# A tile's normed rows in two PSUM banks, the second tile's values in the gate buffer, and thirteen resident weight chunks

## The reference

```python
h = rmsnorm(x, g_mix)
p, q, k, v, gl = split(h @ w_in)              # 512 + 3*512 + 2*1024 columns
branch_a = pool_mixer(p, w_pool, pool_scale)  # trailing means over 2/4/8/16 tokens, per-group map
branch_b = moba_attention(q, k, v) @ w_attn_up  # 8 heads of 64, causal, ALiBi
gates = sigmoid(gl)
x = x + (gates[..., :1024] * branch_a + gates[..., 1024:] * branch_b) @ w_out
xn = rmsnorm(x, g_ffn)
# PEER: per token 8 heads x 16 experts, found by two top-16 searches over 128 keys each
eid, cv = product_key_search(xn @ w_q, sub_keys)
act = gelu(einsum('thkd,td->thk', u[eid], xn))
x = x + einsum('thk,thkd->td', softmax(cv) * act, v[eid])
```

## Time and profile before

| | us |
|---|---|
| median of 3 runs | 1575.68 (1574.5 to 1578.08) |
| the profiled execution: its time | 1575.04 |
| its span, first to last instruction | 1573.3 |
| busy in the span: PE, DVE, ACT, POOL | 1284.6, 1149.6, 914.3, 662.0 |
| bytes over DMA | 643.51 MB, mean 409 GB/s |

### The profile page before, as it was taken

One profiled execution on the slowest core, in us unless ns is written; L12 is line 12 of the kernel. 1 busy time (PEld: TensorE's weight loads), 2 busy tenths in 40 slices (PEclk: granted clock), 3 DMA queues, 4 the chain that ended last, 5 costly groups with the idle time before them and its releaser, 6 DMA issues.

```text
span 1573.3 us, 18796 instructions
## 1 busy us (share of the span) xinstructions
PE 1284.6 (82%) x5582; PEld 788.0 (50%) x5582; DVE 1149.6 (73%) x2692; ACT 914.3 (58%) x3307; POOL 662.0 (42%) x516
## 2 busy tenths in 40 slices
PE   8999898886898788766688978797778888787875
PEld 8986566543554556533355546564445542222321
DVE  2159998877888869636778887976778777777545
ACT  2236566557667546434676664655676666666676
POOL 0014344455445333223554433335554445554552
PEclk9999999997999899986899989999999999999999
DMA  9979999999999999999999999999999999999997
GB/s 393 397 320 401 408 413 420 421 421 422 402 389 408 421 420 421 421 421 419 421 417 410 396 417 422 419 420 421 421 418 416 396 410 421 421 421 421 421 420 292
DMA packets 89742, 643.51 MB, mean 409 GB/s; under 512 B 9976, under 2 KB 10536, under 8 KB 11816
## 3 DMA queue, kind: packets, MB, share of 16 engines
q0 software_dynamic: 73728, 536.90, 82.8%
q1 hardware_dynamic: 15588, 105.18, 16.2%
q10 hardware_dynamic: 324, 0.23, 0.0%
HBM read 641.23 MB, written 1.05 MB: 408 GB/s over the span
## 4 chain that ended last, share of the span: by engine, by line
DMA 43%; PE 26%; DVE 18%; ACT 6%; issue 5%; POOL 2%; SPq 0%; DVEq 0%; POOLq 0%; ACTq 0%
DMA ring<-in_uv,expert 41%; PE ybank L675 13%; PE bank L476 9%; DVE ring L1181 7%; DVE xs L1194 2%; POOL ring L1316 2%; DMA wring<-in_chunks 2%; PE bank L622 1%; ACT wgt L885 1%; ACT diag L895 1%; PE bank L611 1%; ACT th L883 1%; DVE buf L974 1%; DVE picked L977 1%; DVE si L930 1%
## 5 line engine op out<-in xcount | busy, mean ns | idle before, releaser
L1316 POOL DMA_INDIRECT ring<-in_uv,expert x512 | 661.8, 1293 | 890.8 <-PE ybank L675 546.2
L675 PE MATMUL ybank<-ring,diag 128*128 128x512 f32 x1528 | 790.7, 653 | 260.7 <-ACT diag L895 259.8
L1181 DVE SCALAR_TENSOR_TENSOR ring<-ring,tok 128x1024 f32<-128x1024 f32 x512 | 624.4, 1224 | 311.3 <-DMA ring<-in_uv,expert 305.8
L675 PEld LDWEIGHTS ybank<-ring,diag 128*128 128x128 f32 x1528 | 282.4, 200 | 654.6 <-ACT diag L895 417.7
L877 ACT ACTIVATE sq<-dots 128x1 f32<-128x1 f32 x512 | 102.8, 201 | 512.2 <-DVE ring L1181 511.2
L885 ACT ACTIVATE wgt<-th,half_p 128x1 f32<-128x1 f32 x512 | 198.1, 387 | 17.1
L476 PEld LDWEIGHTS bank<-hT,wring 128*128 128x128 f32 x1536 | 186.0, 199 | 35.1 <-issue 31.0
L476 PE MATMUL bank<-hT,wring 128*128 128x128 f32 x1536 | 186.8, 282 | 8.4 <-DMA wring<-in_chunks 8.1
L1194 DVE SCALAR_TENSOR_TENSOR xs<-ring,wgt,xs 128x1024 f32<-128x1024 f32 x128 | 164.0, 1282 | 5.2 <-ACT wgt L885 3.7
L895 ACT ACTIVATE diag<-cst,wgt 128x128 f32<-128x128 f32 x382 | 153.4, 402 | 15.9 <-PE ybank L675 3.6
L883 ACT ACTIVATE th<-arg,dots 128x1 f32<-128x1 f32 x512 | 150.8, 295 | 16.6
(11 more groups left out here) (126 smaller groups left out, 791.8 us busy)
## 6 DMA issues: line engine op xcount, KB each, us to landing
wring<-in_chunks SPq DMA_DIRECT2D x52, 1024.0 KB, 9.6
held<-in_chunks SPq DMA_DIRECT2D x24, 1024.0 KB, 24.8
ring<-in_chunks SPq DMA_DIRECT2D x20, 1024.0 KB, 12.0
ring<-in_uv,expert POOLq DMA_INDIRECT x512, 11.9
xs<-in_x SPq DMA_DIRECT2D x2, 512.0 KB, 4.3
wpool<-in_w_pool SPq DMA_DIRECT2D x2, 512.0 KB, 13.4
trunk_out<-buf SPq DMA_DIRECT2D x4, 256.0 KB, 4.8
ring<-in_pool_scale SPq DMA_DIRECT2D x1, 512.0 KB, 14.3
```

The source lines that it names most:

```text
L675: ins = pe.matmul(ybank[m][:, :], diag[:, nth % DIAGS, :], ring[:, (2 * t + r) % RING, D + m * BANK:D + (m + 1) * BANK], start=(nth == ten ...
L1181: dve.scalar_tensor_tensor(out=ring[:, g % RING, 0:D], in0=ring[:, g % RING, 0:D], scalar=1.0, in1=tok[:, :], op0=ALU.mult, op1=ALU.mult, ...
L1316: pool.indirect_dma_start(ring[:, g % RING, :], None, uv, bass.IndirectOffsetOnAxis(ap=expert[:, at:at + 1], axis=0)).then_inc(row_landed[ ...
```

## The change

- `tok` moves from SBUF to two of the six PSUM banks. The mixing keeps six banks until the first head's scores of window 0, and four from there on. `claimed` now takes the bank whose job is oldest and leaves out those that hold `gain0` and `gain1` of the same window. DVE's dot (L1181 before) takes its second operand from PSUM.
- The second tile's values (`v_sb`'s second half) lie in that quarter of the gate buffer which the fourth gate fills last; the gates move round (`GATE_AT`), the fourth waits for `o`, and ACT copies the third gate out at 26 and the fourth at 26.5 (23 and 26 before). Where window 1's values are made early, they wait in `mix` and ACT copies them once (one ACTIVATE more).
- The freed SBUF holds a thirteenth chunk: `peer_wq`'s seventh. Chunk loads fall from 96 to 94.
- The first window's gain goes into the second slot of `wring`; the chunk that follows in that slot waits for a new semaphore, `first_gained`, which DVE raises when `tok` is made.

```diff
+GATE_AT = (1, 2, 3, 0)
 GELU_C = (2.0 / np.pi) ** 0.5
...
+FIRST_NARROW = "score0b"
...
 W_SLOTS = 2
-HELD = 12
+HELD = 13
 HELD_CHUNKS = range(C_UP, C_UP + HELD)
...
         xs = sb("xs", [P, NT * D])
-        tok = sb("tok", [P, D])
         hT = sb("hT", [P, KC, P])
...
+        first_gain = wring[:, 1, 0:D]
         carry = sb("carry", [P, NG * REACH])
         carried = carry[:, :].rearrange("p (g n) -> p g n", n=REACH)
-        v_sb = sb("v_sb", [P, NT * AW])
+        v_sb = sb("v_sb", [P, AW])
         kT = sb("kT", [P, NA, P])
...
+        next_v = mix[:, 0:AW]
         stat = sb("stat", [P, 2, 3])
...
+        later_v = buf1[:, GATE_AT[NG - 1] * BANK:(GATE_AT[NG - 1] + 1) * BANK]
         pqT = score = buf1[:, :].rearrange("p (a n) -> p a n", a=NHP)
...
-        banks = [ctx.enter_context(nc.psum_tensor(f"bank{i}", [P, BANK], F32)) for i in range(6)]
+        banks = [ctx.enter_context(nc.psum_tensor(f"bank{i}", [P, BANK], F32)) for i in range(4)]
...
+        tok = ctx.enter_context(nc.psum_tensor("tok", [P, D], F32))
+        banks += [tok[:, n * BANK:(n + 1) * BANK] for n in range(2)]
         ybank = [ctx.enter_context(nc.psum_tensor(f"ybank{i}", [P, BANK], F32)) for i in range(2)]
...
         job, reads, freed = {}, [], {}
+        lies_in, last_in = [], {}
...
             engine.wait_ge(bank_full, job[w, name] + 1)
-            return banks[job[w, name] % len(banks)]
+            return banks[lies_in[job[w, name]]]
...
+        def bank_read(n):
+            return reads[n], sum(d is reads[n] for d in reads[:n + 1])
...
-            done = reads[job[w, name]]
-            return done, sum(d is done for d in reads[:job[w, name] + 1])
+            return bank_read(job[w, name])
...
             n = len(reads)
+            these = range(len(banks) if (0, FIRST_NARROW) not in job else 4)
...
+            kept = [last_in.get(i) for i in these if last_in.get(i) in (job.get((w, "gain0")), job.get((w, "gain1")))]
+            i = min((i for i in these if last_in.get(i) not in kept or last_in.get(i) is None),
+                    key=lambda i: last_in.get(i, -1))
             job[w, name] = n
             reads.append(reader)
-            if n >= len(banks):
-                done = reads[n - len(banks)]
-                pe.wait_ge(done, sum(d is done for d in reads[:n - len(banks) + 1]))
-            return banks[n % len(banks)]
+            lies_in.append(i)
+            if i in last_in:
+                pe.wait_ge(*bank_read(last_in[i]))
+            last_in[i] = n
+            return banks[i]
...
                     ins = pe.matmul(b[o:o + DH, c * P:(c + 1) * P],
-                                    v_sb[:, s * AW + hd * DH:s * AW + (hd + 1) * DH],
+                                    (later_v if s else v_sb)[:, hd * DH:(hd + 1) * DH],
                                     softT[:, hd, s * P:(s + 1) * P], start=(s == 0), stop=(s == sources - 1))
             filled("o", ins)
-            yield from cols_by(C_GATE + 6, "gate3", 2)
+            yield from cols_by(C_GATE + 6, "gate3", 2, gate_done)
...
                 if w:
-                    act.wait_ge(expert_ready, experts_of(w - 1, 2 * c + 1))
-                copy_out(f"gate{c}", gates[:, c * BANK:(c + 1) * BANK], flat, ACT.Tanh, 0.5)
+                    act.wait_ge(expert_ready, experts_of(w - 1, 2 * GATE_AT[c] + 1))
+                if c == NG - 1:
+                    act.wait_ge(bank_full, job[w, "o"] + 1)
+                q = GATE_AT[c]
+                copy_out(f"gate{c}", gates[:, q * BANK:(q + 1) * BANK], flat, ACT.Tanh, 0.5, gate_done)
...
             def values(w):
-                mine = v_sb[:, w % NT * AW:(w % NT + 1) * AW]
+                if w > 1 and w % NT:
+                    act.wait_ge(expert_ready, experts_of(w - 1, 2 * GATE_AT[NG - 1] + 1))
+                mine = (v_sb[:, :], next_v, v_sb[:, :], later_v)[w]
                 act.activation(mine, filled_bank(act, w, "v")[:, :], ACT.Copy).then_inc(a_done, 1)
...
             soft_out(3)
-            yield when(w, 23)
-            gate(2)
             yield when(w, 24)
...
             yield when(w, 26)
+            gate(2)
+            yield when(w, 26.5)
             gate(3)
...
                     values(1)
+            if w == 0:
+                yield 6.5
+                act.wait_ge(expert_ready, experts_of(0, 2 * GATE_AT[NG - 1] + 1))
+                act.wait_ge(a_done, read(1, "v")[1])
+                act_stepped(act.activation(later_v, next_v, ACT.Copy))
...
+        act_steps = [0]
...
+        def act_stepped(ins):
+            ins.then_inc(act_step, 1)
+            act_steps[0] += 1
...
                 cols = slice(n * BANK, (n + 1) * BANK)
-                dve.scalar_tensor_tensor(out=merged[:, cols], in0=gates[:, cols], scalar=1.0,
+                q = GATE_AT[n]
+                dve.scalar_tensor_tensor(out=merged[:, cols], in0=gates[:, q * BANK:(q + 1) * BANK], scalar=1.0,
                                          in1=bank(f"pool{n}")[:, :], op0=ALU.add, op1=ALU.mult).then_inc(v_done, 1)
...
                 dve.wait_ge(gain_spread, 16)
-                step(dve.scalar_tensor_tensor(out=tok[:, :], in0=x_of(0), scalar=stat[:, 1, 2:3], in1=tok[:, :],
-                                              op0=ALU.mult, op1=ALU.mult))
-                settle(dve)
+                for i in range(4, len(banks)):
+                    dve.wait_ge(*bank_read(last_in[i]))
+                dve.scalar_tensor_tensor(out=tok[:, :], in0=x_of(0), scalar=stat[:, 1, 2:3], in1=first_gain,
+                                         op0=ALU.mult, op1=ALU.mult).then_inc(first_gained, 1)
+                dve.wait_ge(first_gained, 1)
                 return
...
                         n = slot_turns[w, c]
+                        if n == 1:
+                            sp.wait_ge(first_gained, 1)
                         if n >= W_SLOTS:
...
                             heads(layer)
-                        if w != 1 or c not in NEXT_CHUNKS:
+                        if (w != 1 or c not in NEXT_CHUNKS) and (w or slot_turns.get((w, c)) != 1):
                             chunk(w, c)
...
                         spread = rows[0:1, G_FFN:G_FFN + KC, :].rearrange("o k n -> o (k n)").to_broadcast([P, D])
-                        sp.dma_start(tok[:, :], spread).then_inc(gain_spread, 16)
+                        sp.dma_start(first_gain, spread).then_inc(gain_spread, 16)
+                        if slot_order[1][0] == 0:
+                            chunk(*slot_order[1])
                 for t in range(NT):
```

More of the change, by code:

```diff
@@ L218, in build @@
         gain_spread = sem("gain_spread")
+        first_gained = sem("first_gained")
         next_moved = sem("next_moved")
@@ L230, in build @@
         a_done, v_done = sem("a_done"), sem("v_done")
+        gate_done = sem("gate_done")
         ssq_done = sem("ssq_done")
@@ L562, in tensor_mix @@
             yield from cols_by(C_P, "p", 2, v_done)
-            yield from cols_by(C_GATE, "gate0", 2)
+            yield from cols_by(C_GATE, "gate0", 2, gate_done)
             yield when(w, 16)
@@ L568, in tensor_mix @@
                 everywhere(pe, w, G_POOL, "scale")
-            yield from cols_by(C_GATE + 2, "gate1", 2)
+            yield from cols_by(C_GATE + 2, "gate1", 2, gate_done)
             yield when(w, 19)
@@ L589, in tensor_mix @@
                 filled(f"pool{n}", ins)
-            yield from cols_by(C_GATE + 4, "gate2", 2)
+            yield from cols_by(C_GATE + 4, "gate2", 2, gate_done)
             yield when(w, 23)
@@ L683, in scalar_mix, with copy_out @@
             width = (tile + 1) * P
-            def copy_out(name, dst, view=blocks, func=ACT.Copy, scale=1.0):
-                act.activation(dst, view(filled_bank(act, w, name)), func, scale=scale).then_inc(a_done, 1)
+            def copy_out(name, dst, view=blocks, func=ACT.Copy, scale=1.0, done=a_done):
+                act.activation(dst, view(filled_bank(act, w, name)), func, scale=scale).then_inc(done, 1)
             def flat(b):
```

7 lines of the change are left out of this document (2 added, 5 removed).

## The result

The changed kernel takes 1584.51 us (median of 4 runs, 1583.73 to 1586.21) against 1576.37 of the kernel before beside it: 1.0055 times, 95% interval 1.0041 to 1.0069, or 8.7 us slower by the ratio (8.1 by the two medians). The forecast was 1577.5 us, the range 1570 to 1583, so both missed. The profiled execution has a span of 1581.9 us, 8.6 more than before.

A forecast was written before the change was run, and what follows sets the result against it. DMA bytes bound most of the span (421 GB/s), DVE bound 120 to 230 us. 1575.04 + 2.1 (a) + 0.2 (b) + 0 (c and d) + 0.2 (e) gave 1577.5 us, range 1570 to 1583.

The forecast's parts named there:

- (b): Mixing 1: four banks make gate2 and gate3 wait; the dropped load's saving of 2.5 us is lost, +0.2 us.
- (e): Mixing 3: the same waits as in mixing 1; the dropped load gives +0.2 us in place of -2.5.
- the slack of the ring: Wherever the rate is 421 GB/s, a gather issued up to some 6 us later lands at the same time.
- my 6.2: Mixing 1: gate3 waits for DVE's read of pool0 until 290.2, so it and the rows behind are 6.2 us late.
- The clock's rival: Mixing 1 and 3: PE's clock falls while it waits ahead of gate3, 1.7 us more each; 1581 us, chance 0.20.
- (a): Start: chunk (1,0) loads at about 111 us among the first gathers and delays the fourth dot; +2.1 us net.
- (c): Layer 1's burst of held chunks, 640 to 725 us: the thirteenth chunk costs its full +2.5 us.
- (d): The load at 880.9 us goes, for its full -2.5 us.
- The dots from PSUM: DVE's path, 111 to 230 us: 45 dots each 65 ns longer, +2.9 in place of -0.4; 1580.8 us, chance 0.05.
- The bytes come through: PE's lateness about 2.5 us less than forecast, so the fewer loads pay: 1570.0 to 1572.2 us, chance 0.20.
- The range: 1570 to 1583 us, from the bytes coming through up to the clock's fall with a dearer early load.

The follow-up runs named there:

- r_after: The changed kernel as it is, run and traced again in another session: 1.0052 times the kernel before.
- t4_banks: Kernel before with only the new bank claiming, four banks in place of six; tok in SBUF, 96 loads: 1.0052 times the kernel before, 8.2 us slower.
- v1_late: Changed kernel with the load of chunk (1,0) held back to about 166 us, second run: 1.0035 times the kernel before.
- u3_filler: Changed kernel with PE working in vain while it waits, pool0 and pool1 three times and o twice in windows 1 to 3: 1.0036 times the kernel before.
- t3_soft: Changed kernel with only ACT's copies of gate1 and soft0 to soft3 sooner, at ticks 19 to 21: 1.0030 times the kernel before, 1580.75 us.
- v3_pool: Changed kernel with only DVE's reads of pool0 and pool1 sooner, at ticks 23.5 and 24.5: 1.0001 times the kernel before.
- s3_filler: Changed kernel with PE working in vain while it waits, pool0 and pool1 five times each in windows 1 to 3: 1.0059 times the kernel before, 1582.81 us.
- t2_late_sooner: Changed kernel with chunk (1,0) loaded late, ACT's copies at ticks 19 to 21, DVE's pool reads at 23.5 and 24.5: 1569.51 us, 0.9953 times the kernel before.
- u1_six_sooner: Kernel before (six banks, 96 loads) with ACT's copies at ticks 19 to 21 and DVE's pool reads at 23.5 and 24.5: 1.0001 times the kernel before.
- s4_less: Kernel before (six banks, tok in SBUF) with 94 chunk loads, chunk 28 not loaded in windows 1 and 3: 0.9974 times the kernel before.

## Why the prediction was wrong

**The step that failed is (b)**, and with it its copy (e). It had the right waits at the right places, and priced them at +0.2 us each; the dots show +3.8 in both. (The sum's +0.2 for (b) is also a slip: landing 0.4 us late in place of 2.5 us early is +0.4.) The price hangs on two sizes, the lateness of the rows behind `gate3`, 6.2 us, and the slack of the ring, 6 us, and both were wrong. How late they were in mixing 1, in us behind the kernel before:

| kernel | start of `gate2` | row behind its first chunk | DVE's read of `pool0` | row behind `gate3`'s first chunk | dots at t40 |
|---|---|---|---|---|---|
| changed | 9.9 | 13.0 | 3.6 | 11.5 | 6.8 |
| `r_after` | 9.3 | 11.7 | 3.4 | 12.4 | 7.3 |
| `t4_banks` | 10.1 | 12.6 | 3.6 | 11.5 | 7.4 |
| `v1_late` | 7.5 | 9.6 | 0.4 | 8.2 | 4.1 |
| `u3_filler` | 9.2 | 9.3 | 0.8 | 8.7 | 3.0 |
| `t3_soft` | 3.8 | 3.8 | 1.0 | 8.9 | 3.8 |
| `v3_pool` | 9.9 | 11.7 | 0.0 | 6.2 | 1.8 |

The 11.5 us are my 6.2, the 3.6 by which the read moved, and 1.6 for `gate3`'s slow chunk. Last column against last but one, the ring took up 4.1 to 5.7 us of lateness and not 6: with rows just 6.2 us late, as I had forecast, `v3_pool` still has its dots 1.8 us late. Three statements fell:

- "It started at 284.04: 6.2 us late, whatever came before." I took the end of DVE's read of `pool0` from the trace of before, as if it could not move. It moved by 3.6 us, since it stands behind a dot, the dot waits for a gather, and the gather waits for PE, which was late from `gate2`. The first wait feeds the second through the ring. The table bears it out: the read moves by 3.4 us or more only where the row behind `gate2`'s chunk is 11.7 us late or more, and by 1.0 or less where it is at most 9.6 late; `s3_filler`, not in the table, has 2.2 at 11.8. (In `v3_pool` the read stands elsewhere, ahead of those dots.) So the start and the slow chunk have a part in it too: `v1_late` lacks the early load, `u3_filler` the slow chunk, and in both the read hardly moves. `v3_pool` cuts the loop at the second wait and gets 8 us back, `t3_soft` at the first and gets 3.5.
- "The gathers that the lateness at `gate2` holds back stand in the longer queue of two chunk loads of their own, which come just as late, so I charge nothing for it." The rate from 260 to 280 us fell from 420 to 369 GB/s, 2.4 us at once (351 in `t4_banks`). SP's loads wait for the same late PE, so there was no longer queue.
- `gate2`'s lateness itself, 8.1 us, left out that ACT's copy comes later too (`soft2` 1.8 us) and that the first chunk runs at a low clock. The row at 278.17, which in the order follows `gate2`'s first chunk, started 13.0 us behind that of before (265.21).

Mixing 3 is the same: the read of `pool0` starts at 1065.54, 5.6 us behind before, of which 5.0 had been carried in, and the row behind `gate3`'s first chunk 13.5 us behind. In mixing 1 it was 11.5 with 3.0 carried in, 8.5 us more in either case.

**The clock's rival** (0.20) was the nearest to the truth: 1581, and "slower". Its mechanism is there, but at both places, where I had thought that a fall at `gate2` would spare `gate3`: 3.0 us and 1.6 us in mixing 1 by the chunks' times. `u3_filler` shows about 2.5 us of the result. It is a part only; the cause is the two waits, behind which the clock falls.

**(a) held, mechanism and size**: +2.1 forecast, 2.0 us at the fourth dot by nine traces against nine, and 0.8 to 4.1 us at the end by the runs, none of them sharp. The 3.2 of the first pair of traces was for a third part the chance of a single trace. The dots became 5 ns shorter, not 9, and up to 230 us there are 40 of them, not 45; neither moves the sum.

**(c) and (d), together 0, held**: 0.1 us between ticks 86 and 136, and each shows by itself. From tick 90 to 102, where the thirteenth chunk is loaded, the lateness grows by 2.8 us (2.2 in `r_after`, 2.4 in `t2_late_sooner`); from tick 126 to 138, at the load that goes, it falls by 3.2 (3.1, 3.2). In between `gate3` waits 8.4 us for the read of `pool0`, more than in mixing 1, and it costs nothing that the dots show. The waits that I left out are there too, 4.2 us for DVE's read of `qk0` in mixing 2 and 4.9 us for ACT's copy of the values in mixing 3, where the rate stays at 420 GB/s. What I had not reckoned is that 1.9 us are given back between ticks 40 and 86, where DMA was not full before (396 GB/s from 400 to 500 us, 410 with the change); 1.1 of it is also there in `u1_six_sooner`, so its cause stays open in part.

**The dots from PSUM** (0.05) are refuted, as the rows had it. The Trainium skill's page VectorE: DVE Perf Modes, section The TRN2 errata, makes such a dot 65 ns longer, by the estimate made from its fixed terms. The trace has it 5 ns shorter, and the trace decides.

**The bytes come through** (0.20) is true of six banks (`s4_less`) and of four banks that are read in time (`t2_late_sooner`).

**The range** ended at 1583 because it let the clock and a dearer start add up, but held the lateness at both waits and the slack fixed. That the lateness might grow by itself was not among its cases. That the time came within 1.5 us of the range's end is chance.

## What to carry to other kernels

When a change adds a wait, ask what the releaser itself stands behind in its queue, and whether that depends on the waiter: the time at which it released before is no constant. Before taking buffers away, move their reads forward; here two reads moved ahead by 1.5 and 1 ticks were worth 8 us, and nothing while there were six banks. Here a saving in bytes was collected only where the rows stayed within the ring's slack (4.1 us with six banks, 6.1 with four that are read sooner, 0.3 to 2.7 with four that are not), so price the lateness of the busiest engine first, then the bytes.

## What the runs showed of the hardware

POOL's gather instruction became shorter. The groups of the kernel before and of the changed one:

```profile
L1316 POOL DMA_INDIRECT ring<-in_uv,expert x512 | 661.8, 1293 | 890.8 <-PE ybank L675 546.2 <-DVE xs L1194 200.9 <-DVE expert L985 103.4
```

```profile
L1352 POOL DMA_INDIRECT ring<-in_uv,expert x512 | 503.9, 984 | 1056.8 <-PE ybank L697 731.9 <-DVE xs L1230 185.0 <-DVE expert L1017 103.3
```

1293 and 984 ns; the four kernels with `tok` in SBUF have 1272 to 1304, the fourteen with `tok` in PSUM 972 to 986, whatever their banks. The shortest is 0.93 or 0.94 us in both; what differs is the share of longer ones: above 1.5 us there were 195 of 512, and now there are 17. The dot had two operands in SBUF before and has one now. The Trainium skill's page SBUF — State Buffer, section Who interferes with whom, says that a VectorE instruction with two inputs in SBUF contends with a GpSimd instruction that reads SBUF, and that one with a single input there, outside the 2-port modes, doesn't. The traces agree, for a gather that takes its row numbers from a tile in SBUF (`expert`). It brought nothing that could be told here, since POOL mostly waits for PE.
